# Moving the key, value and tail loads of a hybrid decoder step, and the order of its last four chunks

## What is computed

```python
past = cache_k[layer, page_table[:, :own * ppb]].astype(jnp.float32)
kmean = jnp.mean(past.reshape(DB, own, MOBA_BLOCK, N_HEADS, HEAD_DIM), axis=2).transpose(0, 2, 1, 3)
gate = jnp.einsum('bhtd,bhnd->bhtn', qh.astype(jnp.float32), kmean)
_, sel = lax.top_k(gate, n_sel)
...
x = x + g1 * (jnp.concatenate([attn, pool], axis=-1) @ w_out)
h = rms_norm(x, norm_mlp) * (1 + sc2) + sh2
return x + g2 * (jnp.square(jax.nn.relu(h @ w_up)) @ w_down)
```

## Time and profile before

| what | us |
|---|---|
| median of 3 runs | 891.32 |
| their range | 888.59 to 897.85 |
| the profiled execution | 896.14 |
| its span | 894.3 |
| PE busy | 838.0 |
| DVE busy | 448.7 |
| ACT busy | 338.0 |
| POOL busy | 292.6 |

### The profile page before, as it was taken

The page is one execution under the profiler, slowest core; times in us unless marked ns, Lnnn a source line. Parts: engine busy times, 40 slices in busy tenths (PEclk is TensorE's granted clock), DMA queues, the critical chain, the costliest instruction groups (busy, mean ns, idle before and its releaser), DMA issues.

```text
span 894.3 us, 20195 instructions
## 1 busy us (share of the span) xinstructions
PE 838.0 (94%) x7634; PEld 589.7 (66%) x7634; DVE 448.7 (50%) x845; ACT 338.0 (38%) x701; POOL 292.6 (33%) x191
## 2 busy tenths in 40 slices
PE   5799999898999699999999999999999999997984
PEld 4577786666776176666666676676676675576873
DVE  2743223664777884674674674674674441221222
ACT  4233223787114646136136136036036145133011
POOL 0330003956132444334334334334333353225000
PEclk9899999999999899999999999999999999999998
DMA  9842236595998889999999999999999999899896
GB/s 302 324 154 95 95 115 253 166 337 177 297 312 262 298 279 309 316 315 321 311 316 329 299 321 323 302 310 326 298 325 364 288 309 333 279 326 329 304 397 248
DMA packets 167825, 254.02 MB, mean 284 GB/s; under 512 B 10454, under 2 KB 69419, under 8 KB 167755
## 3 DMA queue, kind: packets, MB, share of 16 engines
q1 hardware_dynamic: 166995, 250.66, 82.9%
q0 software_dynamic: 768, 2.51, 0.8%
HBM read 248.56 MB, written 4.75 MB: 283 GB/s over the span
## 4 chain that ended last, share of the span: by engine, by line
PE 80%; DMA 7%; DVE 6%; issue 2%; ACT 2%; SPq 2%; POOL 0%; DVEq 0%; ACTq 0%
PE PS L1560 77%; DMA W<-in_w_down_dram 3%; DMA W<-in_cache_v_dram 2%; DMA mixT<-in_x_prompt_dram 1%; SPq L500 1%; DMA out_dram<-hT 1%; DVE W L1337 1%; PE PS L1909 1%; PE PS L1783 1%; DMA W<-in_w_up_dram 1%; DVE hT L1116 1%; DVE xT L1405 1%; DVE mixT L1277 0%; DVE stat L1279 0%; POOL hT_split L644 0%
## 5 line engine op out<-in xcount | busy, mean ns | idle before, releaser
L706 POOL TENSOR_TENSOR W_split<-W,W_split 128x1024 fp32r<-128x1024 f32 x72 | 172.3, 2393 | 298.6 <-ACT W_split L866 143.2
L1560 PE MATMUL PS<-gT_split,W_split 128*128 128x512 f32 x576 | 200.9, 408 | 1.0 <-DVE xT L1405 0.2
L1337 DVE STREAM_TRANSPOSE W<-rwT 128x512 f32<-128x512 f32 x256 | 162.6, 681 | 36.5 <-PE PS L1560 22.6
L1560 PE MATMUL PS<-rwT_split,W_split 128*128 128x512 f32 x512 | 175.0, 404 | 0.0
L1560 PE MATMUL PS<-hT_split,W_split 128*128 128x512 f32 x416 | 162.3, 399 | 0.5 <-ACT mixT L939 0.5
L1560 PEld LDWEIGHTS PS<-gT_split,W_split 128*128 128x128 f32 x576 | 109.1, 189 | 53.9 <-DVE xT L1405 17.2
L1560 PEld LDWEIGHTS PS<-rwT_split,W_split 128*128 128x128 f32 x512 | 96.7, 189 | 31.9 <-issue 12.6
L1405 DVE SCALAR_TENSOR_TENSOR xT<-PS,mods,xT 128x512 f32<-128x512 f32 x64 | 47.5, 742 | 110.5 <-PE PS L1560 110.2
L866 ACT ACTIVATE W_split<-W 128x1024 fp32r<-128x1024 f32 x32 | 33.9, 1059 | 179.7 <-DMA W<-in_w_up_dram 179.6
L1560 PE MATMUL PS<-kT_split,W_split 128*128 128x512 f32 x256 | 100.3, 392 | 0.0
L1560 PEld LDWEIGHTS PS<-hT_split,W_split 128*128 128x128 f32 x416 | 79.1, 190 | 16.5 <-issue 1.6
(11 more groups left out here) (273 smaller groups left out, 958.3 us busy)
## 6 DMA issues: line engine op xcount, KB each, us to landing
rwT<-in_cache_k_dram SPq DMA_DIRECT2D x256, 256.0 KB, 4.2
W<-in_cache_v_dram SPq DMA_DIRECT2D x256, 256.0 KB, 4.0
W<-in_w_ada_dram SPq DMA_DIRECT2D x12, 2048.0 KB, 10.3
W<-in_w_up_dram SPq DMA_DIRECT2D x32, 512.0 KB, 5.7
W<-in_w_down_dram SPq DMA_DIRECT2D x32, 512.0 KB, 5.8
W<-in_w_down_dram SPq DMA_DIRECT2D x8, 2048.0 KB, 10.3
rwT<-in_w_up_dram SPq DMA_DIRECT2D x4, 2048.0 KB, 10.0
mixT<-in_w_up_dram SPq DMA_DIRECT2D x4, 2048.0 KB, 11.8
```

Source lines behind the costliest of these rows:

```text
L706: pool.tensor_tensor(rows_part(RAW, q, W_split), rows_part(RAW, q), rows_part(HIGH, q, W_split), ALU.subtract).then_inc(w_low, 1)
L1337: dve.transpose(ktb[u % 2][:, :, g, :], k_ring[:, j % SLOTS, pg, :]).then_inc(kt_ev, 1)
L1560: return pe.matmul(out, lhsT, rhs, start=start, stop=stop, **kw)
```

## The change

The loop ends one turn earlier (i = 0 to 3), and turns 4, 5 and 6 are written out on every engine.

- In turn i = 4, key units (6,6) to (7,7) are loaded, turned and scored: ten are loaded and twelve scored, where a turn of the loop has eight of each. `take_queries(7)` moves on POOL ahead of `up_low(5, 0)`.
- In turn i = 5, no keys are left. All eight value units of sequence 6 are used beside `down(5)`, and all eight of sequence 7 beside `up(6)`, one per group of twelve matmuls. The ranking of sequence 7 stands between the `down(5)` tiles. Tails 0, 1 and 2 are loaded in this turn, between the value units: tail 0 after unit (6,1), tail 1 after (7,1), tail 2 after (7,3) and a quarter.
- From `down(6)` on, the sample's end is interleaved with `down(6)`, `up(7)` and `down(7)`: `sample_out` stands in the first two `down(6)` tiles, steps 0 and 1 among `down(6)`, steps 1 to 3 among `up(7)`, steps 4 to 7 among `down(7)`. The four `final_rows` stand together after the last `down(7)` tile, ahead of `sample_down(7)`; `final_norm` and `final_out` follow in the same way on ACT and DVE.
- SP's list follows these orders: quarters of `up(7)` and `down(7)` come between tails 3 to 13.

```diff
--- before.py
+++ after.py
-            with sp.Fori(0, LAST - 2) as i:
+            with sp.Fori(0, LAST - 3) as i:
...
+            def key_unit(b, u):
+                for j in (PPB * u, PPB * u + 1):
+                    load_keys(b, j)
+
+            def value_unit(b, u):
+                for j in (PPB * u, PPB * u + 1):
+                    load_values(b, j)
+
+            i = LAST - 3
+            key_unit(i + 2, 6)
+            value_unit(i + 1, 1)
+            sp.wait_ge(up_ps, HP * (i + 1))
+            load_down(i, 3)
+            key_unit(i + 2, 7)
+            value_unit(i + 1, 2)
+            sp.wait_ge(dn_ps, FT * i + 2)
+            load_up(i + 1, 0)
+            key_unit(LAST, 0)
+            value_unit(i + 1, 3)
+            sp.wait_ge(dn_ps, FT * i + 4)
+            load_up(i + 1, 1)
+            key_unit(LAST, 1)
+            value_unit(i + 1, 4)
+            sp.wait_ge(dn_ps, FT * i + 6)
+            load_up(i + 1, 2)
+            key_unit(LAST, 2)
+            sp.wait_ge(dn_ps, FT * i + 8)
+            load_up(i + 1, 3)
+            key_unit(LAST, 3)
+            value_unit(i + 1, 5)
+            key_unit(LAST, 4)
+            sp.wait_ge(up_ps, HP * (i + 1) + 1)
+            load_down(i + 1, 0)
+            key_unit(LAST, 5)
+            value_unit(i + 1, 6)
+            sp.wait_ge(up_ps, HP * (i + 1) + 2)
+            load_down(i + 1, 1)
+            key_unit(LAST, 6)
+            value_unit(i + 1, 7)
+            key_unit(LAST, 7)
+            sp.wait_ge(up_ps, HP * (i + 1) + 3)
+            load_down(i + 1, 2)
+            value_unit(i + 2, 0)
+
+            i = LAST - 2
+            sp.wait_ge(up_ps, HP * (i + 1))
+            load_down(i, 3)
+            value_unit(i + 1, 1)
             load_tail(0)
-            for u in range(UNITS):
-                section(LAST - 2, u, keys=u < 2)
-                if u == 5:
+            for q in range(PARTS):
+                value_unit(*((i + 1, 2 * q + 2) if q < PARTS - 1 else (LAST, 0)))
+                sp.wait_ge(dn_ps, FT * i + 2 * q + 2)
+                load_up(i + 1, q)
+                value_unit(*((i + 1, 2 * q + 3) if q < PARTS - 1 else (LAST, 1)))
+            sp.wait_ge(qk, UNITS * DB)
+            load_tail(1)
+            for q in range(PARTS - 1):
+                value_unit(LAST, 2 * q + 2)
+                value_unit(LAST, 2 * q + 3)
+                sp.wait_ge(up_ps, HP * (i + 1) + q + 1)
+                load_down(i + 1, q)
+                if q == 0:
                     sp.wait_ge(kt_ev, PAGES * DB)
                     load_tail(2)
-                    sp.wait_ge(qk, UNITS * DB)
-                    load_tail(1)
             sp.wait_ge(up_ps, HP * LAST)
             load_down(LAST - 1, 3)
-            for j in range(2, 4):
-                load_values(LAST, j)
-            for q in range(PARTS):
-                if q < PARTS - 1:
-                    for j in range(4 * q + 4, 4 * q + 8):
-                        load_values(LAST, j)
-                sp.wait_ge(dn_ps, FT * (LAST - 1) + 2 * q + 2)
-                load_up(LAST, q)
             sp.wait_ge(v_used, BLOCKS * DB)
             load_tail(3)
+            sp.wait_ge(dn_ps, FT * (LAST - 1) + 2)
+            load_up(LAST, 0)
             sp.wait_ge(so_ps, 1)
             load_tail(4)
             load_tail(5)
-            sp.wait_ge(up_ps, HP * LAST + 1)
-            load_down(LAST, 0)
-            sp.wait_ge(up_ps, HP * LAST + 2)
-            load_down(LAST, 1)
+            sp.wait_ge(dn_ps, FT * (LAST - 1) + 4)
+            load_up(LAST, 1)
             sp.wait_ge(sup_ps, 1)
             load_tail(6)
-            sp.wait_ge(up_ps, HP * LAST + 3)
-            load_down(LAST, 2)
+            sp.wait_ge(dn_ps, FT * (LAST - 1) + 6)
+            load_up(LAST, 2)
             sp.wait_ge(sdn_ps, 1)
             load_tail(7)
-            sp.wait_ge(up_ps, HP * LAST + 4)
-            load_down(LAST, 3)
+            sp.wait_ge(dn_ps, FT * (LAST - 1) + 8)
+            load_up(LAST, 3)
             for n in range(8, N_TAIL):
                 sp.wait_ge((sup_ps, sdn_ps)[n % 2], (n - TAIL_SLOTS) // 2)
                 load_tail(n)
+                if n in (9, 11, 12, 13):
+                    q = (9, 11, 12, 13).index(n)
+                    sp.wait_ge(up_ps, HP * LAST + q + 1)
+                    load_down(LAST, q)
...
+                if keys:
+                    take_queries(i + 3)
...
+            front(LAST - 3, keys=True)
+            for i in range(LAST - 3, LAST):
+                back(i, keys=False)
...
+            hidden(LAST - 2, HP - 1)
+            down_high(LAST - 2, 2)
+            probs_out(LAST - 1, 1)
+            down_high(LAST - 2, 3)
+            up_high(LAST - 1, 0)
+            exps(LAST)
+            up_high(LAST - 1, 1)
+            probs_out(LAST, 0)
+            probs_out(LAST, 1)
+            back(LAST - 2, chain=False)
...
+            up_high(LAST, 0)
+            up_high(LAST, 1)
+            sample_relu(0)
+            up_high(LAST, 2)
+            sample_relu(1)
+            up_high(LAST, 3)
+            hidden(LAST, 0)
...
+            sample_relu(2)
             hidden(LAST, 1)
             down_high(LAST, 0)
-            sample_relu(0)
             hidden(LAST, 2)
...
+            for i in range(4, N_CH):
                 sample_relu(i)
-                if i == 5:
-                    final_norm(0)
-                    final_norm(1)
-                elif i > 5:
-                    final_norm(i - 4)
+                if i == N_CH - 1:
+                    for t in range(TT):
+                        final_norm(t)
...
+            turn_keys(LAST, 3)
+            rank_blocks(i + 2)
+            turn_keys(LAST, 4)
+            less_max(i + 2)
+            turn_keys(LAST, 5)
+            turn_keys(LAST, 6)
+            take_total(i + 2)
+            scores_out(LAST, 0)
+            turn_keys(LAST, 7)
+
...
+            sample_copy(0)
+            down_out(LAST - 1, 4)
+            sample_square(0)
+            down_out(LAST - 1, 5)
+            down_out(LAST - 1, 6)
+            sample_copy(1)
+            down_out(LAST - 1, 7)
...
+            sample_copy(4)
+            sample_square(4)
+            down_out(LAST, 0)
+            down_out(LAST, 1)
+            for i in range(5, N_CH):
+                sample_copy(i)
+                down_out(LAST, 2 * i - 8)
+                sample_square(i)
+                down_out(LAST, 2 * i - 7)
+            for t in range(TT):
+                final_out(t)
...
+            i = LAST - 3
+            score_keys(i + 2, 4)
+            down(i, 0, 0, HP - 1)
+            turn_heads(i)
+            down(i, 1, 0, HP - 1)
+            weigh_values(i + 1, 0)
+            down(i, 0, HP - 1, HP)
+            down(i, 1, HP - 1, HP)
+            for u in range(1, 4):
+                down(i, 2 * u)
+                score_keys(*((i + 2, u + 4) if u < 3 else (LAST, 0)))
+                down(i, 2 * u + 1)
+                weigh_values(i + 1, u)
+                if u > 1:
+                    score_keys(*((i + 2, 7) if u == 2 else (LAST, 1)))
+            for u in range(4, UNITS):
+                up(i + 1, u - 4, 0, 4)
+                score_keys(LAST, (2, 3, 5, 6)[u - 4])
+                up(i + 1, u - 4, 4, FT)
+                weigh_values(i + 1, u)
+                if u == 4:
+                    add_sums(i + 2)
+                if u == 5:
+                    spread_max(i + 2)
+                    score_keys(LAST, 4)
+                if u == 6:
+                    total(i + 2)
+                    turn_probs(i + 2)
+                if u == 7:
+                    score_keys(LAST, 7)
+
+            i = LAST - 2
+            down(i, 0, 0, HP - 1)
+            turn_heads(i)
+            down(i, 1, 0, HP - 1)
+            weigh_values(i + 1, 0)
+            down(i, 0, HP - 1, HP)
+            weigh_values(i + 1, 1)
+            down(i, 1, HP - 1, HP)
             for u in range(2, UNITS):
-                down(LAST - 1, u)
-                weigh_values(LAST, u)
+                down(i, u)
+                weigh_values(i + 1, u)
+                if u == 2:
+                    add_sums(LAST)
+                if u == 4:
+                    spread_max(LAST)
+                if u == 6:
+                    total(LAST)
+                    turn_probs(LAST)
+            for u in range(HP):
+                up(i + 1, u, 0, 4)
+                if u == 0:
+                    turn_heads(i + 1)
+                weigh_values(LAST, 2 * u)
+                up(i + 1, u, 4, FT)
+                weigh_values(LAST, 2 * u + 1)
...
+            i = LAST - 1
+            down(i, 0, 0, HP - 1)
             turn_heads(LAST)
+            down(i, 1, 0, HP - 1)
             sample_out()
+            down(i, 0, HP - 1, HP)
+            down(i, 1, HP - 1, HP)
+            fold_out()
+            down(i, 2)
+            sample_mean_square()
+            down(i, 3)
+            sample_up(0)
+            down(i, 4)
+            fold_up(0)
+            down(i, 5)
```

(123 more changed lines are left out.)

54 lines of the change are left out of this document (10 added, 44 removed).

## The result

The changed kernel takes 909.11 us (median of 4 runs, 906.89 to 913.70), the kernel before in the same comparison 893.09: a ratio of 1.018, 95% interval 1.014 to 1.022. It is slower by 16.0 us, where +9.7 was forecast against the median; the range of 883 to 911 held it. The profiled execution took 908.48 us. First the page's first line, then the stretches (columns as in the earlier trace rows; the last four rows are short stretches inside the others).

A forecast was written before the change was run, and what follows sets the result against it. PE was taken to bound the kernel, with DMA close under it. The terms, 1.7 + 9 - 3 + 6 + 0 - 9.3 + 5, gave +9.4 on a span of 894.3, so 903.7, or 901 against the median; range 883 to 911.

The forecast's parts named there:

- keys ahead: Turn five: PE scores twelve key units and waits for DVE's late transposes behind the ranking, +1.7 us, between 0 and 2.5.
- values ahead, less the 3 of before: Turn six: value units wait for loads queued with three tails, 9 us (3 to 13), minus 3 us of earlier waits.
- the sample's start: Ahead of `sample_down(0)`: relu behind a late quarter's conversion, wait 4.5 us plus 1.5 of lower clock, +6, between 0 and 9.
- the "4.88 us wait": Ahead of `sample_down(4)`: ACT's relu behind `down_high(LAST, 3)` in the same order as before, wait taken as unchanged, 0.
- the last stage: From 862.0 to 885.6 in the kernel before: waits of 7.6 us and 1.7 of clock go, -9.3.
- the pile: At the end: four `final_rows` together ahead of `sample_down(7)` lie in the open, +5 us, between 2.5 and 6.5.
- R3: Whole change: the waits add up, every term at its upper end, +18.7, 910 us; chance 0.16.
- R1: Turn six and the sample's start: the queue keeps up, so not slower, -2.8, 888.5 us; chance 0.22.
- R2: R1, and the wait of 4.88 us goes too, a further 4.88 + 1.7, 882 us; chance 0.12.

The follow-up runs named there:

- b_keys: The kernel before with only the keys moved ahead (turn five as in the changed kernel, values and end as before): 895.57 us, ratio 1.003.
- light tails: Tails 0, 1 and 2 loading an eighth of their bytes: 901.37 us in the changed kernel's own order, 888.41 us with both `sample_relu` ahead of the conversions.
- a_relu: The changed kernel with `sample_relu(0)` and `sample_relu(4)` each put ahead of a weight conversion on ACT: 895.14 us, ratio 1.002.
- a_light0: The changed kernel in its own order, with tails 0, 1 and 2 loading an eighth of their bytes: 901.37 us, ratio 1.011.
- b_relu: The kernel before with `sample_relu(1)` put ahead of `down_high(LAST, 3)` on ACT: 887.82 us, ratio 0.9935.
- a_best: The changed kernel with both relus ahead, tail 2 behind the values, the end reordered, and two transposes earlier on DVE in turn five: 890.09 us, ratio 0.997.
- a_pile: The changed kernel with `sample_down(7)` ahead of the `final_rows` on PE and the sample's copy and fold ahead of `final_out` on DVE: 909.50 us, ratio 1.017.

## Why the prediction was right or wrong, by its steps

The side held, though it had been given only 0.45 against 0.43 for no change, and so did most of the mechanisms; the size did not. Term by term, in us (measured in the traces):

| step | forecast | measured | seen in |
|---|---|---|---|
| keys ahead | +1.7 | +2.6 | three waits; b_keys +2.3 |
| values ahead, less the 3 of before | +6 | +7 to +8 | 79.2 for 68.5 of work; light tails 7.4 less |
| the sample's start | +6 | +6.5 | a_relu |
| `hTs` late at `sample_up(0)` | none | +0.6 | 1.42; before 0.78, for ACT's `hTs` |
| the "4.88 us wait" | 0 | +2.1 | 8.7 with its clock, before 6.6 |
| `sample_down(3)` | none | +0.7 | 0.73 at 836.75 |
| the last stage | -9.3 | -9.3 | no wait from 860 to 887 |
| the pile | +5 | +5 | 0.84 + 2.27 + 1.16, and clock |
| sum | +9.4 | +15 to +16 | 14.8 |

**Keys.** Right in place, and above the upper end of 2.5: in the traces with this order the waits are 2.1 to 3.4 us. I counted the two units behind the ranking; a third, at 650.9, waits as well, because its transposes stood waiting for the key load.

**Values.** The turn was to be short by three tails, and it was, by 7.4 and 10.6 us with the tails full against light ones. It took 79.2 us for 68.5 of work, 10.7 of waits where I took 9. Taking 3 us off for before was right to within the spread of a turn of 2 us. The lower clock that I counted for R3 only was there: 0.71 at 740 to 744, behind a wait of 2.45 us in two parts.

**The sample's start.** A quarter landing "near 28" us behind the last value unit, a wait of 3.7 to 5.8: counted from that unit's end, as I did, the conversion began at 28.5, PE wanted the product at 27.5 and not at 26, and the wait was 4.79.

**The step that failed** is "I take it as unchanged: 0", the 4.88 us wait. The order was a copy, its surroundings were not: the wait was 7.13. The load behind it took 9.64 us where I carried over 7.41, and these 2.23 us are the whole difference of 2.25; the lower clock behind the wait cost 1.6 us, before 1.7. The queue was fuller when the load was issued. In the changed kernel SP sends three pieces of 2 MB and three quarters between 825 and 842 without a pause (DMA share 1.05 in the row above), and the quarter before `load_down(LAST, 3)` is 11.5 us on its way (833.17 to ACT's 844.71). In the kernel before, the 17 us ahead of that load had this row:

```profile
797.00:814.00 17.00, 17.00 (x193) 13.97 (x193) 3.13 (x6) 7.30 (x11) 7.29 (x4) 1.00 0.89 312
```

That the fuller queue made the load longer is read from these rows; no run moved the load within the queue. The wait at `sample_down(3)`, which I did not count, has nothing to do with it: it is 0.73 or 0.74 us also in a_relu and in a_light0. ACT's relu stands there behind `hidden`, and DVE's square takes 1.30 beside a subtraction on POOL (835.18, 1.28 long):

```profile
835.29 1.30 DVE L1655 TENSOR_TENSOR gS<-gS 128x128 f32<-128x128 f32 x1 [4.75 <-ACT gS L1097]
```

Of the 5.4 us that were missing, the 4.88 us wait is 2.1, the values 1 to 2, the keys 0.9, `sample_down(3)` 0.7 and `hTs` 0.6: the terms meet the measured 14.8 to about 1 us.

**The rivals.** R1 and R2 are out: value units waited, and both ACT waits stayed. R3, every term at its upper end (910), comes near the time by luck, not by its sum: the start and the pile came in at the main case, and the 4.88 us wait, which made up for part of that, is 0 in R3 too. The values were done by 764, as forecast; that did not bring the end nearer, because `down(6)` and the whole sample's end still had to follow, and there each of the two relus stood behind a load.

What I passed over is the more useful finding. I read the 4.88 us wait in the trace of before, named its cause, and priced it as something that the change leaves alone; two lines moved on ACT take it away. In b_relu that makes the kernel before 5.8 us faster, and in a_relu it pays back 14 of the 16 us that the change had cost.

## What to carry to other kernels

Where an in-order engine converts a late weight and then does a small step that everyone waits for, put the small step first; a wait that the trace puts down to a vector operation may be a load three steps behind it. A wait that is copied with its order is to be priced anew, by how full the queue will be when its load is issued. And when a load is moved out of one starved stretch, look at what stands behind its new place: tail 2 moved its 3 us into the next wait until that one was gone.

## What the hardware showed that I had not expected

DVE's square of 128x128 takes 2.37 us at 794.18 in the changed kernel, and 0.28 in a_relu, where no subtraction runs on POOL then. In the changed kernel two operations of one other shape take 0.43 and 2.48, and the second stands beside POOL's, which began 0.07 us behind the first. The first fence is the timeline of the changed kernel (DVE, POOL, DVE), the second that of a_relu (DVE, POOL, DVE):

```profile
781.14 0.43 DVE L1222 TENSOR_TENSOR hTs<-hTs,mod_a 128x256 f32<-128x256 f32 x1
781.60 2.48 DVE L1223 TENSOR_TENSOR hTs<-hTs,mods 128x256 f32<-128x256 f32 x1
...
781.21 2.58 POOL L758 TENSOR_TENSOR W_split<-W,W_split 128x1024 fp32r<-128x1024 f32 x1 [9.96 <-ACT W_split L919]
...
794.06 2.34 POOL L758 TENSOR_TENSOR W_split<-W,W_split 128x1024 fp32r<-128x1024 f32 x1 [10.27 <-ACT W_split L919]
...
794.18 2.37 DVE L1655 TENSOR_TENSOR gS<-gS 128x128 f32<-128x128 f32 x1 [4.36 <-ACT gS L1097]
```

```profile
793.23 0.28 DVE L1656 TENSOR_TENSOR gS<-gS 128x128 f32<-128x128 f32 x1
...
843.10 2.39 POOL L758 TENSOR_TENSOR W_split<-W,W_split 128x1024 fp32r<-128x1024 f32 x1 [1.14 <-ACT W_split L1025]
843.24 2.39 DVE L1656 TENSOR_TENSOR gS<-gS 128x128 f32<-128x128 f32 x1 [2.36 <-ACT gS L1097]
```

DVE's operation ends just after POOL's each time (784.08 after 783.79, 796.55 after 796.40). So some 2 us of each of the two waits, 4.79 and 7.13, came from the conversion's second half on POOL, and the 2.48 us operation made the wait of 1.42 at `sample_up(0)`. Putting the relu first took the square of `sample_down(0)` out from under POOL; that of `sample_down(4)` met the subtraction of the quarter before and took 2.39 in a_relu as well, which left the wait of 0.80 there. The Trainium skill, "SBUF — State Buffer", section Who interferes with whom, has it that a DVE operation with both inputs in this memory and a POOL operation that reads it block each other, the later one until the first is done; the rows agree.

A gap of one length lowered the clock in one execution and not in another. Behind a gap of 2.46 us at the end, 16 transposes took 3.33 us in a_best (its row of PE's timeline follows; granted clock 0.61 from 879.9 to 883.3), and eight took 1.06 in a_pile above (1.00 from 894.5 to 895.6). Behind gaps of 4.7 us and more ahead of a sample product, that product took 3.2 to 3.6 us in all of these traces.

```profile
879.95 3.33 PE L2297 MATMUL PS<-cst,xT 128*128 128x128 f32 x16 [2.46 <-DVE W L1643]
```
